# Gated linear attention: where in its order ScalarE squares a finished head's output

## The reference

```python
def _gla_chunkwise(q, k, v, lf, S):
    ...
        b = jnp.cumsum(lfc, axis=2)
        o = jnp.einsum('bhtk,bhkv->bhtv', qc * jnp.exp(b), S)
        pair = jnp.exp(jnp.where(tri, b[:, :, :, None, :] - b[:, :, None, :, :], -jnp.inf))
        a = jnp.einsum('bhtk,bhtsk->bhts', qc, pair * kc[:, :, None, :, :])
        o = o + jnp.einsum('bhts,bhsv->bhtv', a, vc)
...
    def merge(o, z):
        o = _rms(jnp.swapaxes(o, 1, 2).astype(z.dtype), h_norm.reshape(HG_HEADS, HG_VDIM))
        return (o.reshape(o.shape[:2] + (HG_VW,)) * jax.nn.silu(z)) @ w_out
```

## Time and profile before

| | |
|---|---|
| Time, median of three runs | 2541.75 us (2539.33 to 2545.14) |
| Profiled execution, its own time | 2545.83 us |
| Its span, first to last instruction | 2544.2 us |
| TensorE, matmuls | busy 2341.7 us (92%) |
| VectorE | busy 1699.2 us (67%) |
| ScalarE | busy 1105.7 us (43%) |
| Mean granted TensorE clock | 0.945 |
| TensorE idle before L1247 | 65.3 us in 32 instructions, released by ScalarE L1874 |

### The profile page before, as it was taken

One profiled execution on the slowest core, in us unless ns is written; L12 is line 12 of the kernel. 1 busy time (PEld: TensorE's weight loads), 2 busy tenths in 40 slices (PEclk: granted clock), 3 DMA queues, 4 the chain that ended last, 5 costly groups with the idle time before them and its releaser, 6 DMA issues.

```text
span 2544.2 us, 37779 instructions
## 1 busy us (share of the span) xinstructions
PE 2341.7 (92%) x13692; PEld 2024.7 (80%) x13692; DVE 1699.2 (67%) x3262; ACT 1105.7 (43%) x1761; POOL 88.8 (3%) x140
## 2 busy tenths in 40 slices
PE   7999899998999889987999999999978898889878
PEld 7998689987998679976777778888857787778768
DVE  6787758777777867765445554345437777877784
ACT  4333443344343443344555533344325555455552
POOL 0000000000000000002122101111000000000000
PEclk9999789998999889998999989999989999999889
DMA  7654135554653135634344412212112122112212
GB/s 271 218 196 155 58 135 211 197 191 148 229 203 138 56 138 193 226 145 66 68 82 74 91 66 75 67 58 81 44 66 83 66 82 74 66 66 82 74 50 100
DMA packets 81765, 298.62 MB, mean 117 GB/s; under 512 B 10132, under 2 KB 10644, under 8 KB 80916
## 3 DMA queue, kind: packets, MB, share of 16 engines
q1 hardware_dynamic: 77904, 284.72, 31.8%
q0 software_dynamic: 2048, 4.20, 2.9%
q10 hardware_dynamic: 1736, 8.67, 0.9%
HBM read 296.51 MB, written 1.05 MB: 117 GB/s over the span
## 4 chain that ended last, share of the span: by engine, by line
PE 43%; DVE 7%; ACT 3%; issue 1%; DVEq 0%; ACTq 0%
PE ps L711 33%; PE ps L1303 2%; PE ps L1162 1%; PE ps L1044 1%; PE ps L1058 1%; ACT wsplit L1359 1%; PE ps L1034 1%; DVE work L2684 1%; DVE work L2615 1%; DVE work L2627 1%; DVE work L2613 1%; PE ps L1247 1%; PE ps L1014 1%; PE ps L1281 1%; DVE work L2618 0%
## 5 line engine op out<-in xcount | busy, mean ns | idle before, releaser
L711 PE MATMUL ps<-hsplit,wsplit 128*128 128x256 f32 (+1 forms) x8280 | 1407.8, 329 | 23.7 <-DVE hsplit L2308 11.6
L711 PEld LDWEIGHTS ps<-hsplit,wsplit 128*128 128x128 f32 x8280 | 1221.0, 194 | 160.9 <-DVE hsplit L2308 12.2
L1966 DVE TENSOR_TENSOR wsplit<-ring,wsplit 128x1024 fp32r<-128x1024 f32 x465 | 569.9, 1228 | 350.6 <-ACT wsplit L1359 340.0
L1359 ACT ACTIVATE wsplit<-ring 128x1024 fp32r<-128x1024 f32 x465 | 491.5, 1059 | 615.3 <-PE ps L711 431.5
L753 PE MATMUL ps<-wsplit,fsplit 128*128 128x512 f32 x1056 | 267.0, 403 | 19.8 <-DVE wsplit L1966 14.2
L753 PEld LDWEIGHTS ps<-wsplit,fsplit 128*128 128x128 f32 x1056 | 199.6, 195 | 59.7 <-DVE wsplit L1966 14.9
L2014 DVE SCALAR_TENSOR_TENSOR work<-ring,cs,work 128x128 f32<-128x128 f32 x672 | 206.2, 349 | 9.0
L2120 DVE SCALAR_TENSOR_TENSOR work<-work,vec 128x256 f32<-128x256 f32 x240 | 101.0, 488 | 1.7
L711 PEld LDWEIGHTS ps<-wsplit,hsplit 128*128 128x128 f32 x768 | 96.1, 199 | 5.3 <-issue 3.8
L1456 ACT ACTIVATE work<-ps 128x256 f32<-128x256 f32 x88 | 33.8, 384 | 152.3 <-PE ps L711 152.3
L711 PE MATMUL ps<-wsplit,hsplit 128*128 128x256 f32 x768 | 97.7, 290 | 1.1 <-DVE wsplit L1966 1.1
(11 more groups left out here) (321 smaller groups left out, 2382.8 us busy)
## 6 DMA issues: line engine op xcount, KB each, us to landing
ring<-panels SPq DMA_DIRECT2D x539, 512.0 KB, 4.2
work<-latent_weights ACTq DMA_DIRECT2D x2, 2304.0 KB, 13.2
work<-rpb POOLq DMA_DIRECT2D x64, 64.0 KB, 6.8
cst<-constants ACTq DMA_DIRECT2D x1, 1408.0 KB
work<-x SPq DMA_DIRECT2D x1, 1024.0 KB, 5.2
work<-post_rows ACTq DMA_DIRECT2D x2, 512.0 KB, 5.8
cT<-ctx ACTq DMA_DIRECT2D x1, 1024.0 KB, 9.8
out<-xT SPq DMA_DIRECT2D x1, 1024.0 KB, 3.9
```

The source lines that it names most:

```text
L711: ins = mm(out_, w(a), x(b), start=start and n == 0, stop=stop and n == 2, **kw)
L1359: af(wsplit[:, split_slot(name, n), 0, :], ring[:, p % slots, :], ACT.Copy).then_inc(high_ready, 1)
L1966: tt(parts[:, 1, :], ring[:, p % slots, :], parts[:, 0, :].bitcast(fp32), ALU.subtract)\
```

## The change

ScalarE's `c_square(h - 1)`, with the wait for `c_o_done` that it holds, is issued as the first thing of a head's list, before the exponential at L1885, and no longer between the copy at L1895 and the exponential at L1898. The other engines' lists stay as they are, as does `c_factor`.

```diff
             def c_head(h, par, n0, nx, more=True, before=True):
 
+                if before:
+                    c_square(h - 1)
                 act.wait_ge(c_t_ready, h + 1)
                 af(c_kl[:, :, :], c_x[:, :, 0:T], ACT.Exp, scale=-1.0)
                 act.wait_ge(c_qz_in, h + 1)
...
                 high("C", 0, nx[0] + 1, nx[1])
                 act.wait_ge(panels_used, n0 + 5)
                 af(c_vT, ps[:, 3, :], ACT.Copy).then_inc(c_vT_ready, 1)
-                if before:
-                    c_square(h - 1)
                 af(c_qs[:, :, :], c_b[:, :, 0:T], ACT.Exp).then_inc(c_eb_ready, 1)
                 if before:
                     c_factor(h - 1)
```

## The result

The changed kernel takes 2558.39 us (median of five, 2549.53 to 2561.91) against 2542.31 us for the kernel before: a ratio of 1.006, with a 95% interval of 1.0037 to 1.0082. It is 16 us slower, where the prediction had worked out 14.5.

The account below looks back on a forecast made before the run. In the linear attention TensorE waits for ScalarE's square, then for VectorE's low part of panel 1, with clock falls on top. Sum -21.2 + 35.7 + 0 + 0 = +14.5 us: 2560.3 from the profiled 2545.83, 2556 from the median; range 2530 to 2568.

Parts of the forecast that it names:

- The second wait: TensorE cannot begin panel 1 before VectorE's low part (L1966), which was to end no earlier, 7.62 us after the first half panel.
- T: The moment when TensorE ends the first half panel of a pass, from which the prediction counts its times.
- The gap: TensorE's idle time, moved from before the mean to before panel 1: 4.6 us a pass in place of 3.75.
- The gain up to the start of panel 1, -21.2 us: Gain at an equal clock: 21.73 us between low part's end and panel 1, less 14 starts of about 0.04 us.
- The 1.55 us of room a pass: Time per pass from the end of panel 1's low part on VectorE to panel 1's start on TensorE, 21.73 us in sum.
- The clock over panel 1, +35.7 us, 2.55 a pass: Cost of the granted clock falling to 0.5 behind the new gap, over panel 1: mean 2.55 us, 35.7 in 14 passes.
- three kinds of stretch: Low-clock stretches starting 2.0, 3.0 or 3.6 us after the gap's start, all taken as 6.8 us long.
- ScalarE's list, 0: ScalarE's first exponential (L1885) starts under 0.5 us late, hidden by 1.3 us idle before L1891: cost nothing, upper bound 7 us.
- The last head, 0: Head without projection: the cross product (L1289) waits for VectorE's L2663 anyway, so nothing gained, at most 1.68 us.
- The pass: T to T in the linear attention: 36.35 us before, about 37.4 after the change.
- The rival on the other side: The clock does not fall behind the new gap, or hardly: -21.2 us, 2520.5 from the median; chance 0.11.

Follow-up runs that it names:

- the first two experiments: Panel 1's low part before the key differences on VectorE: in the changed kernel 2491.9 us, ratio 0.9814; in the kernel before 2537.62 us, ratio 1.0003.
- The filled run of the changed kernel: Changed kernel plus five matmuls nothing reads, on TensorE before panel 1 in each of 14 passes: 2516.38 us, ratio 0.992 to the kernel before.
- The old order filled: Kernel before plus four matmuls nothing reads, on TensorE in front of the mean in each of 14 passes: 2520.16 us, ratio 0.9929.
- the first experiment: Changed kernel with panel 1's low part issued before the eight key differences on VectorE: 2491.9 us, ratio 0.9814 to the kernel before.
- The run with the square in the third place: Changed kernel with the square moved behind the sigmoid, before ScalarE's wait for L2627: 2557.8 us, ratio 1.0077 to the kernel before.
- the low part in the middle: Changed kernel with panel 1's low part behind four of the eight key differences on VectorE: 2519.02 us, ratio 0.9929 to the kernel before.

## Why the prediction was right

*The second wait.* T to the end of the low part was to stay 7.62 us a pass. It is 106.58 us in 14 passes after the change, against 106.64. That it is this wait which binds is shown by the pair of the first two experiments, since moving the low part changes the time only when the square is early. The prediction's reason, that VectorE's list before it hangs on nothing that moves, holds to 0.1 us.

*The gap.* 4.6 us was forecast, and 62.55 / 14 = 4.47 measured. TensorE is done with the second half panel at T + 3.20 (pass 3) and not at T + 3.08.

*The gain up to the start of panel 1, -21.2 us.* From T to the start of panel 1 it was 106.64 + 21.73 = 128.37 us in 14 passes, and it is 107.35 now: -21.0. The filled run of the changed kernel, in which no low clock takes any of it back, is 20 us under the kernel before (2537.11 x 0.0080). But the prediction was wrong to call this a gain at an equal clock. The old order filled gains as much, 18 us (x 0.0071), and at a full clock in both orders the square's place is worth nothing. The 1.55 us of room a pass between the low part's end and panel 1 were themselves made by the low clock over the mean and the second half panel; at the full clock TensorE comes 0.47 us before the low part is there. So the change did not trade a gain in waiting against a loss of clock: it moved the low clock from work that partly lay under the cover of the low part to panel 1, where nothing covers it.

*The clock over panel 1, +35.7 us, 2.55 a pass.* Panel 1 takes 113.51 us in 14 passes against 76.47 before, +37.0, or 2.65 a pass. Filling the gap takes it away. With the -21.0 that makes +16.0 us. Not all of the 37.0 is the clock: in the 11 passes of the first experiment in which the clock stayed up, panel 1 took 5.58 to 5.62 us behind its gap, where it took 5.46 in one row with the second half panel. By that some 2 us in 14 passes (an estimate) are the start behind a gap, a term that the prediction did not have, and some 35 are the clock. The pattern behind the number was right in length and wrong in spread: I shifted three kinds of stretch, costing 2.1, 2.6 and 2.9 us (their mean is 2.53, which gives 35.5 and not 35.7), and got a short stretch in pass 0 and one kind from pass 1 on, 6.8 us long with 5.3 to 5.7 us of it on work. That the short stretch of pass 0 took back some 1 us of the missing term is luck. The Trainium skill (TensorE: Matmul & The Clock Gate, HAM oscillation — how this bites in real kernels) says that a wait in each round starts the next group of matmuls cold in each round. The trace agrees in 13 of 14 passes; in pass 0 panel 1 started at 1951.16 at the full clock, and the clock fell at 1952.00. The Trainium skill's price for it on the same page (Terms), half of the throttled time, would be 91.80 / 2 = 45.9 us, and half of TensorE's busy time in those stretches is 75.49 / 2 = 37.7; the measured growth of panel 1, 37.0, stands with the second.

*ScalarE's list, 0.* In pass 3 the square starts at 2052.22 and the first exponential at 2052.50, 2.42 us before T where it was 2.82 before T: 0.4 us later, with under 0.5 forecast. ScalarE is still idle before L1893, 14.3 / 14 = 1.0 us a pass. The run with the square in the third place has the same 37.44 us a pass without this delay, so the delay costs nothing.

*The last head, 0.* From the end of L1316 of pass 13 to the cross product it is 21.15 us before and 21.13 after (2461.47 to 2482.62 before; 2465.03 to 2486.16 now), though the mean comes 1.58 us behind it and no longer 12.38:

```profile
2464.00 1.03 PE L1316 MATMUL ps<-work 128*128 128x256 f32 x4
2466.61 0.70 PE L1247 MATMUL ps<-work,ones 128*128 128x256 f32 x2 [1.58 <-ACT work L1874]
...
2486.16 1.22 PE L1289 MATMUL ps<-work 128*128 128x128 f32 x4 [1.84 <-DVE work L2663]
```

*The pass.* 37.4 us was forecast, 37.44 measured. The rival on the other side, that the clock holds, did not come; its price of -21.2 us was right, as the filled run of the changed kernel shows.

## What to carry to other kernels

Before a wait is removed, look for what becomes due right behind it, and write down by how much that was early; here it was 1.5 us a pass against a gap of 3.75, and the removal moved the gap instead of closing it. Ask of such room what makes it, too: here it was the low clock behind the gap, and it was gone once the clock stayed up. Price the place where a gap will stand too: a gap in front of small work and one in front of the largest group of matmuls cost differently when the clock falls behind it. Two moves that are each worth nothing or less can be worth 45 us together, so a move that fails should be tried once more with the next wait in line moved as well.

## What the hardware showed that I had not expected

The passes of the kernel before took 35.5 to 37.1 us, in a pattern of three; those of the changed kernel from pass 1 on are all 37.3 to 37.7 us, with the lower clock always 6.8 us long. The run with the square in the third place repeats this: a short stretch in pass 0, 6.8 us in the 13 others. A change that alters the length of a gap can thus leave a loop in the dearest of its patterns; why it settles there no run shows.

The fall of the clock has no sharp bound in the gap's length: gaps of 3.6 us and over were followed by it every time (28 of 28 in the two kernels), gaps of 2.9 to 3.2 us in 12 of 14 passes, and the six gaps of about 1.9 us in the first experiment still in 3. Its eight gaps of 1.6 us were followed by none. Nor does the length alone decide: with the low part in the middle all eight gaps of 2.9 us made the clock fall, and two of the six of 3.2 us did not. And matmuls that compute nothing of use shortened the kernel by 18 to 20 us, only by keeping the clock up.
